# Decode products, scores and copies at other places, softplus in halves, a third row buffer earlier, and word gathers paced, in a one-core hybrid decoder step

## The reference

```python
h = rmsnorm(x, g);  q, k, v, glu, gate_a, gate_c = split(h @ w_in)       # 2048 x 9216
z = (q . k) / 8 + bias                                                  # stick-breaking attention, 16 heads
log_1m = where(visible, log_sigmoid(-z), 0);  tail = suffix sums of log_1m
attn = where(visible, exp(log_sigmoid(z) + tail), 0) @ v                # decode rows read paged K and V
conv = silu(layernorm(depthwise_conv31(glu_a * sigmoid(glu_b))))
x += (sigmoid(gate_a) * (attn @ w_pa) + sigmoid(gate_c) * (conv @ w_pc)) @ w_o
h = rmsnorm(x, g2);  s = (h @ w_query) . sub_keys                       # 8 heads x 2 x 128 scores
idx, gate = top 16 of the sums of the top 16 of each half, softmax      # 8 x 16 experts of 16384 a token
x += sum(gate * gelu(h . expert_u[idx]) * expert_v[idx]);  y = rmsnorm(x, gf)
```

## Time and profile before

| what | us |
|---|---|
| timed runs | 2226.40, 2231.97, 2233.87 |
| median | 2231.97 |
| the profiled execution | 2224.84 |
| its span in the trace | 2223.1 |
| TensorE matmuls busy | 2190.8 (99%) |
| weight loads busy | 2144.8 (96%) |
| VectorE busy | 1663.0 (75%) |
| ScalarE busy | 1213.6 (55%) |
| GpSimd busy | 685.8 (31%) |
| mean granted TensorE clock | 0.992 |

### The profile page before, as it was taken

One profiled execution on the slowest core, in us unless ns is written; L12 is line 12 of the kernel. 1 busy time (PEld: TensorE's weight loads), 2 busy tenths in 40 slices (PEclk: granted clock), 3 DMA queues, 4 the chain that ended last, 5 costly groups with the idle time before them and its releaser, 6 DMA issues.

```text
span 2223.1 us, 55796 instructions
## 1 busy us (share of the span) xinstructions
PE 2190.8 (99%) x16578; PEld 2144.8 (96%) x16578; DVE 1663.0 (75%) x3039; ACT 1213.6 (55%) x2217; POOL 685.8 (31%) x516
## 2 busy tenths in 40 slices
PE   9999999999999999999999999999999999999997
PEld 8999999999999999999999999999999999999997
DVE  8777788887766667888885444476778887888887
ACT  6445366667455445555555444455555665556564
POOL 0221100002011000788888888300245222111120
PEclk9999999999999999999999999999999999999998
DMA  7887756666556556788876888698789998899984
GB/s 241 280 294 238 244 184 214 204 214 218 184 180 208 171 169 181 189 179 188 189 178 166 210 186 182 174 335 267 241 253 317 336 328 292 273 293 293 301 284 176
DMA packets 337994, 514.37 MB, mean 231 GB/s; under 512 B 87276, under 2 KB 126564, under 8 KB 337772
## 3 DMA queue, kind: packets, MB, share of 16 engines
q1 hardware_dynamic: 263244, 427.59, 61.2%
q0 software_dynamic: 58016, 71.54, 12.9%
q10 hardware_dynamic: 16640, 14.16, 2.0%
HBM read 487.87 MB, written 25.24 MB: 231 GB/s over the span
## 4 chain that ended last, share of the span: by engine, by line
PE 74%; DVE 1%; issue 1%; ACT 0%; DMA 0%; SPq 0%; DVEq 0%; ACTq 0%
PE ps L2167 18%; PE ps L314 15%; PE ps L317 15%; PE ps L313 15%; PE ps L2171 10%; PE ps L2191 0%; PE ps L1394 0%; DMA raw<-u_tiles 0%; DVE lo L301 0%; ACT hi L296 0%; DVE x L2148 0%; DVE whl L2029 0%; PE ps L2200 0%; DVE fin_r L374 0%; DVE x L2089 0%
## 5 line engine op out<-in xcount | busy, mean ns | idle before, releaser
L301 DVE TENSOR_TENSOR lo<-raw,hi 128x512 fp32r<-128x512 f32 x1504 | 1025.6, 694 | 466.4 <-ACT hi L296 333.1
L296 ACT CAST hi<-raw 128x512 fp32r<-128x512 f32 x1504 | 923.1, 620 | 731.9 <-PE ps L317 378.0
L313 PE MATMUL ps<-h_hi,hi 128*128 128x264 f32 (+1 forms) x3200 | 822.3, 286 | 1.5 <-DVE h_lo L950 1.5
L314 PE MATMUL ps<-h_lo,hi 128*128 128x264 f32 (+1 forms) x3200 | 820.8, 286 | 0.0
L313 PEld LDWEIGHTS ps<-h_hi,hi 128*128 128x128 f32 x3200 | 602.4, 188 | 8.9 <-issue 5.7
L314 PEld LDWEIGHTS ps<-h_lo,hi 128*128 128x128 f32 x3200 | 602.6, 188 | 0.0
L317 PE MATMUL ps<-h_hi,lo 128*128 128x264 f32 (+1 forms) x3200 | 524.2, 286 | 6.2 <-DVE lo L301 6.2
L1729 POOL DMA_INDIRECT w_spill<-chosen,widx x256 | 439.7, 1718 | 267.6 <-DVE widx L1951 188.8
L2167 PE MATMUL ps<-whl,hi 128*128 128x432 f32 x2048 | 492.4, 362 | 5.0 <-issue 2.4
L317 PEld LDWEIGHTS ps<-h_hi,lo 128*128 128x128 f32 x3200 | 445.0, 188 | 8.4 <-DVE lo L301 8.4
L2167 PEld LDWEIGHTS ps<-whl,hi 128*128 128x128 f32 x2048 | 350.4, 191 | 14.6 <-issue 4.4
(11 more groups left out here) (302 smaller groups left out, 1729.4 us busy)
## 6 DMA issues: line engine op xcount, KB each, us to landing
raw<-u_tiles SPq DMA_DIRECT2D x512, 256.0 KB
raw<-expert_v SPq DMA_DIRECT2D x512, 256.0 KB
raw<-weights SPq DMA_DIRECT2D x480, 256.0 KB
w_spill<-zeros ACTq DMA_DIRECT2D x16, 864.0 KB, 6.1
wld<-w_spill SPq DMA_DIRECT2D x32, 432.0 KB, 4.3
qb<-q_spill POOLq DMA_DIRECT2D x8, 512.0 KB
w_spill<-chosen,widx POOLq DMA_INDIRECT x256
u_spill<-ust SPq DMA_DIRECT2D x128, 24.0 KB
```

The lines of the kernel that those rows point to most:

```text
L296: nc.scalar.copy(hi[k % SPLIT][:], raw_quarter(k)).then_inc(hi_done, 1)
L301: nc.vector.tensor_tensor(lo[k % SPLIT][:], raw_quarter(k), hi[k % SPLIT][:].bitcast(F32), ALU.subtract).then_inc(lo_done, 1)
L313: pe.matmul(out, a, rhs[0][:, first + j, 0:n], start=start and j == 0, stop=False)
L314: pe.matmul(out, a, rhs[1][:, first + j, 0:n], start=False, stop=False)
```

## The change

**Decode.** `page_products` moves from the second to the fourth quarter of a tile, `page_sums` from the fourth to the second of the next tile; in pair PAIR_SOFT the bias, Abs, Exp and Ln come two or more quarters later. **Attention.** `softplus` and `softplus_lo` are each done in two halves of 896 columns, after the second and the third quarter instead of whole after the third; the semaphore counts follow. The copy `vn` moves from VectorE (in `keep_values`) to ScalarE, four tiles later. STATE_AT moves 2 to 4, 10 to 12, 18 to 20, and so `state_newest` from tile 22 to 24 (1, 6, 9, 14 and 17 stay). **Query stage.** The first `scores` come after the fourth quarter of their tile instead of before it, all later ones before the fourth quarter instead of the third. **Row gathers.** The third buffer is used from row 32 (THREE) on instead of from row 48. **Word gathers.** Those of the second group were two behind each row gather (four behind the first), unpaced; now each waits for its own count of `mm_done`, one to two quarters, and rows 0 and 1 go out with none between them. Nothing of the computation changes.

The diff, with one line of context:

```diff
--- before.py
+++ after.py
@@ -467,8 +467,10 @@
     TAPS_IN = 3 * [7, 6, 6, 4, 4, 4, 6, 7] + [8, 8, 7, 5, 4, 4, 6, 2]
-    STATE_AT = [1, 2, 6, 9, 10, 14, 17, 18]
+    STATE_AT = [1, 4, 6, 9, 12, 14, 17, 20]
     assert sum(TAPS_IN) >= TAPS_LEFT and len(STATE_AT) == KC
+
+    ZCOLS = [slice(0, (ZW + ZM) // 2), slice((ZW + ZM) // 2, ZW + ZM)]
 
...
@@ -710,17 +712,17 @@
                     split_hi(act, 8 * i, AHEAD + r)
-                    if i == PAIR_SOFT and r == 1:
+                    if i == PAIR_SOFT and r == 3:
                         act.wait_ge(d_vec, 1)
                         nc.scalar.activation(ed[:], zd[:], ACT.Abs).then_inc(d_act, 1)
-                    if i == PAIR_SOFT and r == 3:
-                        act.wait_ge(d_act, 1)
-                        nc.scalar.activation(ed[:], ed[:], ACT.Exp, scale=-1.0).then_inc(d_act, 1)
                 tile_done(act, i, 0)
...
                     split_hi(act, 8 * i, 4 + AHEAD + r)
-                    if i == PAIR_SOFT and r == 1:
+                    if i == PAIR_SOFT and r == 0:
+                        act.wait_ge(d_act, 1)
+                        nc.scalar.activation(ed[:], ed[:], ACT.Exp, scale=-1.0).then_inc(d_act, 1)
+                    if i == PAIR_SOFT and r == 2:
                         act.wait_ge(d_act, 2)
...
@@ -754,12 +756,17 @@
                 hi_one(t + 3, 1)
-                act.wait_ge(sp_ready, g + 1)
+                act.wait_ge(sp_ready, 2 * (g + 1))
                 nc.scalar.copy(sp_hi[:], e[:]).then_inc(sp_parts, 1)
...
                 out(t + 3)
-                gate_tile(t + 4)
+                for r in range(4):
+                    hi_one(t + 4, r)
+                    if r == 1:
+                        act.wait_ge(vt_ready, g + 1)
+                        nc.scalar.copy(vn[:].rearrange("p a j n -> p (a j n)"), ps[:, 5, :]).then_inc(vn_ready, 1)
+                out(t + 4)
                 hi_one(t + 5, 0)
...
@@ -847,7 +854,7 @@
                 parts = sp_hi, sp_lo
-                pe.wait_ge(sp_parts, 2 * (g + 1))
+                pe.wait_ge(sp_parts, 3 * (g + 1))
                 for b in range(2):
...
@@ -1074,11 +1081,12 @@
                     split_lo(dve, 8 * i, AHEAD + k)
-                    if b < DEC and k % 4 == 1:
+                    if b < DEC and k % 4 == 3:
                         page_products(b, k // 4)
-                    if b < DEC and k % 4 == 3:
-                        page_sums(b, k // 4)
-                    if i == PAIR_SOFT and k == 0:
+                    last = 2 * b + k // 4 - 1
+                    if 0 <= last < NP and k % 4 == 1:
+                        page_sums(last // PAGES, last % PAGES)
+                    if i == PAIR_SOFT and k == 2:
                         dve.wait_ge(zd_done, NP)
...
@@ -1141,8 +1149,6 @@
             def keep_values(g):
-                dve.wait_ge(vt_ready, g + 1)
-                nc.vector.tensor_copy(vn[:].rearrange("p a j n -> p (a j n)"), ps[:, 5, :]).then_inc(vn_ready, 1)
                 dve.wait_ge(zm_ready, g + 1)
...
@@ -1155,14 +1161,17 @@
 
-            def softplus(g):
+            def softplus(g, part_of):
                 dve.wait_ge(ln_done, g + 1)
-                nc.vector.scalar_tensor_tensor(out=e[:], in0=z[:], scalar=0.0, in1=e[:], op0=ALU.max,
+                cols = ZCOLS[part_of]
+                nc.vector.scalar_tensor_tensor(out=e[:, cols], in0=z[:, cols], scalar=0.0, in1=e[:, cols], op0=ALU.max,
                                                op1=ALU.add).then_inc(sp_ready, 1)
 
-            def softplus_lo(g):
-                dve.wait_ge(sp_parts, 2 * g + 1)
-                nc.vector.tensor_tensor(sp_lo[:], e[:], sp_hi[:].bitcast(F32), ALU.subtract).then_inc(sp_parts, 1)
+            def softplus_lo(g, part_of):
+                dve.wait_ge(sp_parts, 3 * g + 1)
+                cols = ZCOLS[part_of]
+                nc.vector.tensor_tensor(sp_lo[:, cols], e[:, cols], sp_hi[:, cols].bitcast(F32),
+                                        ALU.subtract).then_inc(sp_parts, 1)
 
...
@@ -1222,16 +1231,16 @@
                             one_tap(o)
-                        if r == 2:
-                            softplus(g)
+                        if r in (1, 2):
+                            softplus(g, r - 1)
                 elif t - 4 in Z_AFTER:
...
                             one_tap(o)
-                        if r == 2:
-                            softplus_lo(g)
+                        if r in (1, 2):
+                            softplus_lo(g, r - 1)
                 else:
...
@@ -1399,13 +1408,14 @@
 
-        def query_tile(i, b, at=2):
+        def query_tile(i, b, at=3):
             pe.wait_ge(tile_free[b], i + 1)
...
                 quarter_products(pe, 8 * i, 4 * b + r, ps[:, b, 0:LIVE], raw2, QT * r, LIVE, r == 0, r == 3)
-        query_tile(PAIR_OUT, 1, 3)
+        query_tile(PAIR_OUT, 1, None)
+        scores(PAIR_OUT, 0)
         with pe.Fori(PAIR_OUT + 1, PAIR_QRY) as i:
...
@@ -1566,9 +1576,15 @@
 
+    THREE = 4 * (LATE - FIRST)
+
     def row_slot(n):
 
-        return n % 2 if n < TG else (n - TG) % 3
+        return n % 2 if n < THREE else (n - THREE) % 3
+
+    def slot_uses(n):
+
+        return n // 2 if n < THREE else (n - THREE) // 3 + (THREE // 2 if row_slot(n) < 2 else 0)
     assert HEAD_SPLITS % 4 == 0 and PAIR_S[-1] == PAIR_R and PAIR_R + 5 - PAIR_QRY <= SPARE_PAIR
...
@@ -1748,15 +1764,18 @@
             gather_u(j)
+        words = 0
         for n in range(TG):
             if n >= 2:
-                pool.wait_ge(gat_used, n)
+                while words < min(2 * n + 5, GROUPS[1]):
+                    pool.wait_ge(mm_done, 2 * C0 + SPLIT + 3 * GROUPS[0] + 2 * words)
+                    gather_u(GROUPS[0] + words)
+                    words += 1
+            if n >= 2 and n != THREE + 2:
+                pool.wait_ge(gat_used, n if n < THREE + 2 else n - 1)
             gather_rows(n)
-            for j in range(2 * n + 2 if n else 0, min(2 * n + 4, GROUPS[1])):
-                gather_u(GROUPS[0] + j)
         for n in range(TG, 2 * TG):
-            if n != TG + 2:
-                pool.wait_ge(gat_used, n if n < TG + 2 else n - 1)
+            pool.wait_ge(gat_used, n - 1)
             gather_rows(n)
...
@@ -2057,7 +2076,7 @@
                     j = 4 * (i - FIRST) + LATE_ADDS[i - LATE].index(k)
-                    add_rows(group_of(j), j, j, j % 2, j // 2)
+                    add_rows(group_of(j), j, j, row_slot(j), slot_uses(j))
             elif p == 0 and weighed_groups[0] and k % 2 == 0:
...
@@ -2072,8 +2091,8 @@
                     dve.wait_ge(gacc_zero, 2)
-                add_rows(1 - m // 2, TG + 3 * i + m, GROUPS[0] + 2 * i + m if m < 2 else i, m,
-                         i + (TG // 2 if m < 2 else 0))
+                add_rows(1 - m // 2, TG + 3 * i + m, GROUPS[0] + 2 * i + m if m < 2 else i,
+                         row_slot(TG + m), i + slot_uses(TG + m))
             if p == 1 and static and i == LATE + 1 and k % 4 == 0:
...
```

## The result

The changed kernel takes 2215.47 us (median of 6 runs, 2209.92 to 2218.39) against 2230.32 us for the kernel before (median of 6, 2226.40 to 2233.87). The ratio, estimated from all the runs, is 0.9919, 95% interval 0.9896 to 0.9943; that of the two medians alone is 0.9933. So the kernel is faster by 0.7 to 0.8%, 15 us by the medians. The forecast was 2214.8, 17.2 us under the 2231.97 that the kernel before then had as its median. The profiled execution took 2212.60 us, 12.2 less than the profiled one of before.

The account below looks back on a forecast made before the run. TensorE, busy 99%, bounds the kernel; only late operands and the low clock behind them can be won. 3.9 + 1.5 + 1.5 + 4.5 + 0.8 + 5.0 = 17.2 us off the 2231.97 median gives 2214.8, range 2205 to 2229.

Parts of the forecast that it names:

- Decode products: First decode product near 81 us: moved two quarters later, TensorE's 2.23 us stall and low clock go; 3.9 us, bounds 2.9 to 4.0.
- The cover of 0.6 us: First decode product: the next `lo` ready at 83.8 us, needed at about 84.4, so the stall goes with 0.6 us to spare.
- Softplus: Attention groups: moved state convolutions gain 2.0 us over three second stalls, halving costs 0.5; net 1.5 us, bounds 0.5 to 3.5.
- Query: Query scores: one quarter ahead of each removes the first wait and leaves 0.6 us of the second; 1.46 us, bounds 0.8 to 2.1.
- Words, first part: `expert_v` near 1619 us: pacing word gathers removes a 2.4 us TensorE stall and low clock; 4.5 us, bounds 0 to 4.7.
- The slower rival: Word gathers: a pace of 2.44 us is too dense and holds the loads, 31 us lost, 2250 us; chance 0.05.
- Words, second part: 1637 to 1712 us: words evenly spread remove part of TensorE's 1.22 us idle; 0.8 us, bounds 0 to 1.5.
- Third buffer: End of pass one: rows issued one add earlier, waits go and sums fall to about 3.5 us; 5.0 us, bounds 1.5 to 5.5.
- rival (3): End of pass one: rows issued earlier also land later, adds wait as before; 2219.8 us, chance 0.06.
- rival (4): Row 34, right behind row 33, pushes the weight loads by 1.6 us, 3.3 with low clock; 2218.1 us, chance 0.04.
- rival (1): Waits go but the clock falls anyway, because short waits remain; loses 1.6 + 1.7 + 3.3, 2221.4 us, chance 0.10.
- A long wait costs its own length and then some 1.7 us more.: TensorE stalls: idle over 2 us brings some 3.4 us at 1.2 GHz instead of 2.4, adding some 1.7 us.

Follow-up runs that it names:

- after_again: The changed kernel unaltered, profiled a second time with three more timed runs; ratio to the kernel before 0.9909, profiled execution 2208.74 us.
- decode_alone: Kernel before with only the decode products, sums and softplus steps moved; median 2225.44 us against 2229.59, ratio 0.9977 (0.9952 to 1.0001).
- old_decode: Changed kernel with the decode products, sums and softplus steps back in their old places; ratio to the kernel before 0.9935 (0.9911 to 0.9960).
- even_whole: Changed kernel with softplus and softplus_lo whole again and words from the tenth on two quarters later; 2207.24 us, ratio to the kernel before 0.9888.
- state_alone: Kernel before with only the state convolutions moved (STATE_AT 2, 10, 18 to 4, 12, 20); attention groups 207.8 us against 210.4, no timed ratio given.
- query_alone: Kernel before with only the query scores a quarter later; their waits 0.64 us against 2.10, no timed ratio given.
- three_alone: Kernel before with only the third row buffer from add 32 on; ratio to the kernel before 0.9962 (0.9940 to 0.9984).

## Why the prediction was right, and where not

- **Decode products, 3.9 us.** Shown for the stretch itself. S1 is 65.0 us on average in the seven kernels with the old places (63.7 to 67.3), 61.0 in all seven with the new ones: 4.0. The cover of 0.6 us was thin: the product started at 82.45 us, and TensorE didn't wait; in after_again it started at 82.83, and TensorE waited 0.13. The start scatters from 79.8 to 83.3 us with the new places and from 81.9 to 84.3 with the old, so the delay that I feared from the two added loads isn't seen. What I hadn't counted is where a stream that is ahead arrives next. It is a small matter: pages cost 1.0 us on average in the six kernels with the new places and pages undivided, 0.6 in the seven with the old ones, from 0 to 2.1 and from 0 to 1.3. From thirteen profiles a cause in the move can't be shown. Over S1 and S2 together the averages are 258.7 us with the old places and 255.3 with the new, so 3.4 of the 4.0 reach 280 us; and the timings of decode_alone and old_decode don't set the move apart from nothing. The low clock at pick_heads was 6.8 us long in all seven profiles with pages at 0.6 us or more, and in two of the seven with less.
- **Softplus, 1.5 us.** The direction of each half was right and both sizes were a little off: the second stalls went whole, with the time in which the pipeline refills, 2.6 us instead of 2.0, and the halves cost 0.6 instead of 0.5. Sum 2.1. The `vn` copy is worth nothing, as forecast: even_whole, which has it moved, has the S3 of state_alone, which hasn't (207.8).
- **Query, 1.46 us.** Measured 1.46 in query_alone. The 0.6 us that were to remain are 0.23 and 0.41.
- **Words, first part, 4.5 us.** Shown: S5 is 17.1 us on average with the old order in six kernels (15.7 to 19.0) and 12.2 in all seven with a pace of two quarters, 4.9. The slower rival, a pace too dense, is off even at one quarter. But my reason, "it is the weight loads that come late", was wrong. I had set the profile's releaser aside because TensorE had long finished the quarters in question. It had, and yet its signal was what came late. In the kernel before the weights for the splits at 1616.94 and 1619.83 had landed at 1611.89 and 1613.30. What both splits waited for is the count of `mm_done` for two quarters that TensorE ended at 1614.59 and 1615.81 (its timeline below); by the trace's semaphore events the counts arrived at 1616.92 and 1619.80, 2.3 and 4.0 us later, and each split started 0.03 us behind its count. Until 1611 us counts arrive at once.

```profile
1613.99 0.60 PE L2171 MATMUL ps<-whl,lo 128*128 128x216 f32 x4
1615.22 0.59 PE L2171 MATMUL ps<-whl,lo 128*128 128x216 f32 x4
```

  All ten splits that ScalarE starts after over 1.5 us of idle between 1600 and 1712 us begin 0.02 to 0.03 us behind such a count; for the eight whose landing the trace ties to them the weights had been there for 1.5 us or more. That pacing the words takes the stall away is shown; why TensorE's counts arrive late while POOL issues gathers back to back is not.
- **Words, second part, 0.8 us.** Wrong. "The same number of words evenly spread" was not what the change does there: each word's point had passed when it got its turn, so the pairs stayed. S6 is 70.4 us on average in the six kernels with the old order (68.6 to 73.3), 72.3 in the five with the pace of the change (69.1 to 78.6), a difference inside the scatter. The changed kernel's own profile has no wait of TensorE over 0.15 us there, and 69.1 us. I priced what the wait says, and didn't follow POOL's queue to see whether it still waits.
- **Third buffer, 5.0 us.** The waits of VectorE are gone at the end of pass one in all eight kernels that have it, as forecast, so rival (3) is off; rival (4) isn't seen either: S7, in which row 34 goes out, is 166.6 us in five of the eight and was 166.8 to 168.0 with two buffers. S8 is 16.4 us on average with two buffers in six kernels (14.1 to 18.7), 12.6 with three in eight (11.5 to 14.9): 3.8. The 5.0 in the changed kernel's own profile is in part luck: no stretch of low clock came where I had counted one, and the wait for the accumulator grew from 0.49 to 1.56 us. In four of the eight the clock was low in that stretch all the same, for 3.4 us twice and 10.2 us twice. That is rival (1) at one of its three places. The wait for the accumulator, which I took to stay, is, in these eight, 0.49 us with 10.2 us of low clock ahead of it, 0.99 and 1.27 with 3.4, and 1.56 with none, and gives back a part of what the sums win.
- **"A long wait costs its own length and then some 1.7 us more."** True on the whole, not always: of seven stalls at 81 us (2.03 to 4.65 us) five had the low clock behind them, of six at 1620 us five, of the fourteen of 2.0 us at 510 us, which no kernel changed, eleven. And a wait is not the only way to low clock, which my sum left out outside the sparse sums: pick_heads has it in all fourteen profiles with no wait ahead (timeline of the kernel before, low for 3.4 us from 275.2).

```profile
271.10 3.63 PE L909 MATMUL ps<-sel,vm 128*128 128x4 f32 x32
```
- **The median.** I took the difference of 7.1 us between profiled execution and median as unattributed and forecast from the median. The table suggests what it is: stretches that run well or badly in one execution or the next. With 4.0 + 2.1 + 1.46 + 4.9 + 3.8 = 16.3 us from the averages, the two timings of the changed kernel (14.9 and 18.4 us by medians) lie on either side; this sum leaves out S2 and S6, whose averages went the other way by 0.7 and 1.9 us, inside their scatter. So the median came out within 1 us of the forecast by luck as well: five parts of the sum were off by up to 1.2 us each and the sixth wasn't won at all, and three more runs of the kernel before moved its median from 2231.97 to 2230.32, so that 14.9 us won stand against 17.2 forecast.
- **The range.** "All bounds at their best" give 4.0 + 3.5 + 2.1 + 4.7 + 1.5 + 5.5 = 21.3 us, not 19.3; the lower end of 2205 still covers it.

What stays open: why TensorE's counts arrive late in a burst of gathers; why a set of pages lands 10.3 us after the first one's issue in one place or execution and 13.4 in another; and whether the later words are what made S6 run at 68.6 us without a wait in two of two kernels, since three_alone, with the old order, did so too and state_alone had a single wait of 0.23 us.
